# Tails of three weight units by token block ahead of two more layers, a scaled input in halves, norm weights moved into weights

## What is computed

```python
# first block, twice: x += 0.5*ffn(norm(x)); x += mixer(norm(x)); x += 0.5*ffn(norm(x))
#   first mixer: Mamba-2 ("mamba"), second: latent attention ("mla")
def _short_conv_mixer(h, w_in, w_conv, w_out):          # layer "conv"
    u = h @ w_in                                        # 1024 -> 4 x 1024
    b_gate, c_gate, xin, g = jnp.split(u, 4, axis=-1)
    y = b_gate * _causal_depthwise_conv(c_gate * xin, w_conv)   # 3 taps along tokens
    return (y * jax.nn.silu(g)) @ w_out
# layer "conv":  x = x + _short_conv_mixer(_rmsnorm(x, norm_a), w_in_a, conv_a, w_out_a)
# layer "stick": kv = _rmsnorm(x, norm_kv) @ w_kv       # k, v: 2 x 512
#                q, g = split(_rmsnorm(x, norm_b) @ w_in_b)
#                o = stick_breaking_attention(q, k, v)  # 8 heads of 64
#                x = x + (o * silu(g)) @ w_out_b
# end:           return _rmsnorm(x, norm_f)
def _rmsnorm(x, g):
    return x * rsqrt(mean(x * x) + eps) * g
```

## Time and profile before

| | |
|---|---|
| median of three runs | 1408.57 us (1407.95 to 1410.07) |
| profiled execution, its own time | 1409.99 us |
| its span in the trace | 1408.2 us |
| mean granted clock of PE | 0.968 of full |
| PE busy | 1327.6 us, 94% |
| DVE, ACT, POOL busy | 772.2, 673.6, 132.9 us |
| weights read | 216.82 MB, 155 GB/s over the span |

### The profile page before, as it was taken

How to read it: one execution, slowest core, us unless ns; L and a number is a source line. 1 busy time by engine, 2 the same in 40 slices (tenths; PEclk the granted TensorE clock), 3 DMA queues, 4 the chain that set the end, 5 groups by cost and what they waited for, 6 DMA issues and landing times.

```text
span 1408.2 us, 18444 instructions
## 1 busy us (share of the span) xinstructions
PE 1327.6 (94%) x7004; PEld 1130.8 (80%) x7004; DVE 772.2 (55%) x918; ACT 673.6 (48%) x878; POOL 132.9 (9%) x224
## 2 busy tenths in 40 slices
PE   6999999998889999999999998789999998997977
PEld 5888878997668888888888887678888878996965
DVE  4655545778656555545555445555555545664552
ACT  5544446664546544435444437545554334434441
POOL 3000001036540000000000004500000000000000
PEclk9999999999889999999999999989999999998989
DMA  8665534552125555563655634041755664653301
GB/s 277 196 192 190 202 120 152 179 179 87 63 90 187 172 179 179 179 231 116 221 179 181 232 121 150 30 121 60 239 179 179 209 179 120 180 180 120 120 1 45
DMA packets 179726, 218.78 MB, mean 155 GB/s; under 512 B 8553, under 2 KB 132782, under 8 KB 179662
## 3 DMA queue, kind: packets, MB, share of 16 engines
q1 hardware_dynamic: 179374, 217.75, 47.7%
q0 software_dynamic: 288, 0.15, 0.1%
HBM read 216.82 MB, written 1.05 MB: 155 GB/s over the span
## 4 chain that ended last, share of the span: by engine, by line
PE 85%; DVE 6%; ACT 4%; issue 2%; POOL 2%; DMA 0%; SPq 0%; POOLq 0%; ACTq 0%; DVEq 0%
PE acc L559 26%; PE acc L561 25%; PE acc L560 25%; PE tr L576 3%; DVE w_lo L1668 2%; ACT w_hi L1173 1%; ACT xT_hi L1181 1%; PE tr L807 1%; PE aux L949 1%; DVE conv L1864 1%; DVE xT_lo L1677 1%; DVE E L1822 0%; DMA raw<-in_ffn_w_up 0%; PE aux L1065 0%; PE aux L1066 0%
## 5 line engine op out<-in xcount | busy, mean ns | idle before, releaser
L1668 DVE TENSOR_TENSOR w_lo<-raw,w_hi 128x2048 fp32r<-128x2048 f32 (+1 forms) x207 | 465.8, 2278 | 212.7 <-ACT w_hi L1173 212.7
L1173 ACT ACTIVATE w_hi<-raw 128x2048 fp32r<-128x2048 f32 (+1 forms) x207 | 385.5, 1901 | 135.5 <-PE acc L561 126.9
L559 PE MATMUL acc<-w_hi,xT_hi 128*128 128x512 f32 (+1 forms) x898 | 361.8, 403 | 19.1 <-DVE hT_lo L1677 8.0
L561 PE MATMUL acc<-w_hi,xT_lo 128*128 128x512 f32 (+1 forms) x898 | 354.1, 394 | 0.0
L560 PE MATMUL acc<-w_lo,xT_hi 128*128 128x512 f32 (+1 forms) x898 | 353.8, 394 | 0.0
L559 PEld LDWEIGHTS acc<-w_hi,xT_hi 128*128 128x128 f32 x898 | 173.4, 193 | 55.3 <-DVE hT_lo L1677 8.5
L561 PEld LDWEIGHTS acc<-w_hi,xT_lo 128*128 128x128 f32 x898 | 172.5, 192 | 36.6
L560 PEld LDWEIGHTS acc<-w_lo,xT_hi 128*128 128x128 f32 x898 | 173.6, 193 | 33.6
L559 PE MATMUL acc<-w_hi,hT_hi 128*128 128x512 f32 x448 | 176.4, 394 | 3.4 <-DVE hT_lo L1677 2.6
L560 PE MATMUL acc<-w_lo,hT_hi 128*128 128x512 f32 x448 | 175.1, 391 | 0.0
L561 PE MATMUL acc<-w_hi,hT_lo 128*128 128x512 f32 x448 | 175.1, 391 | 0.0
(11 more groups left out here) (277 smaller groups left out, 1226.4 us busy)
## 6 DMA issues: line engine op xcount, KB each, us to landing
raw<-in_ffn_w_gate SPq DMA_DIRECT2D x88, 512.0 KB, 4.3
raw<-in_ffn_w_up SPq DMA_DIRECT2D x88, 512.0 KB, 5.5
raw<-in_ffn_w_down SPq DMA_DIRECT2D x88, 512.0 KB, 4.8
raw<-in_ssm_w_in SPq DMA_DIRECT2D x48, 512.0 KB, 4.7
raw<-in_w_in_a SPq DMA_DIRECT2D x64, 256.0 KB, 4.1
raw<-in_ssm_w_out SPq DMA_DIRECT2D x16, 512.0 KB, 4.3
raw<-in_mla_w_out SPq DMA_DIRECT2D x8, 512.0 KB, 4.6
raw<-in_w_out_a SPq DMA_DIRECT2D x8, 512.0 KB, 4.7
```

The source lines that it names most:

```text
L559: pe.matmul(o, lh, rh, start=start, stop=False, skip_group_check=skip)
L561: return pe.matmul(o, ll, rh, start=False, stop=stop, skip_group_check=skip)
L1173: act.activation(w_hi[:, u % RING, 0:n], raw[:, u % RING, 0:n], ACT.Copy).then_inc(hi_ready, 1)
L1668: dve.tensor_tensor(w_lo[:, u % RING, 0:n], raw[:, u % RING, 0:n], w_hi[:, u % RING, 0:n].bitcast(F32), ALU.subtract).then_inc(lo_ready, 1)
```

## The change

- `SCALED` = mamba, conv, stick. What held for mamba now holds for all three: `deep` is 3 ahead of them, the turn of block 0 stands before the last part of the tail, DVE takes the low parts of block 0 in its `sums`, one half behind each block's residual, and ACT splits the next layer's second unit between the squares and the scaling of block 0.
- `xn` is written in two instructions of 512 for each block, and PE's turn waits for each half by itself (mamba too).
- conv's first step is computed by token block, as tokens by features (`token_unit`, 48 matmuls of 512 columns, in `first_step`). ACT copies the results from the accumulators to `ct`, PE transposes `ct` back (eight transposes, between the two units of step f = 1), ACT copies one half and DVE the other to `ft`, and f = 1's convolution reads `ft`.
- stick's inputs are transposed without norm weights, one instruction of 512 for each half on ACT and on DVE. The norm weights go into the weights: of stick's first eight units (`w_kv`, `w_in_b`) ACT writes `w_hi` in four instructions of 512 with a column as scale, DVE `w_lo` in four.

```diff
+SCALED = ("mamba", "conv", "stick")
+def weight_norm(u):
+    n = u - sum(len(UNITS_OF[name.rstrip("0123")]) for name in PHASES[:-1])
+    return None if not 0 <= n < 8 else (NORM_KV, NORM_B)[n // 4] + 4 * (n % 2)
...
# PE, input_turns
-                        if half == 0:
-                            c.scaled += 1
-                            pe.wait_ge(xn_ready, c.scaled)
+                        c.scaled += 1
+                        pe.wait_ge(xn_ready, c.scaled)
# PE, first_step
+                k = c.turn - 2
                 early = unscaled(c.name)
-                k = c.turn - 2 if early else c.turn
-                if not early:
-                    input_turns(c.name, 0)
# PE, sum_units
-                deep = 3 if c.next == "mamba" else 2
+                deep = 3 if c.next in SCALED else 2
...
-                    if (n, tb) == (n_u - 1, 1) and (c.next == "mamba" or c.next != "end" and unscaled(c.next)):
+                    if (n, tb) == (n_u - 1, 1) and c.next != "end":
                         input_turns(c.next, 0)
# PE, short_conv
+                first_step(lambda half, tb: token_unit(c.unit + half, c.pair, 4 * half, 4, KD, 512, tbs=(tb,),
+                                                       done=tb == 1, mark=first_half if half else None))
...
+                        if f == 1 and half == 0:
+                            for tb in range(TB):
+                                acc_done(pe, p_first, tb)
+                                turn([(g * P, ct[:, tb, g * P:(g + 1) * P]) for g in range(4)], c.turn)
+                                c.turn += 1
# ACT, split
-                act.activation(w_hi[:, u % RING, 0:n], raw[:, u % RING, 0:n], ACT.Copy).then_inc(hi_ready, 1)
+                    for k in range(4):
+                        at = slice(512 * k, 512 * k + 512)
+                        inst = act.activation(w_hi[:, u % RING, at], raw[:, u % RING, at], ACT.Copy, scale=col(norm + k))
# ACT, layer_input
-                        if tb == 0 and c.name == "mamba":
+                        if tb == 0:
                             split_to(c.unit + 2)
                         act.wait_ge(rstd_ready, c.norm)
-                            act.activation(xn[:, tb, :], x[:, tb, :], ACT.Copy, scale=rstd[:, tb:tb + 1])\
+                        for half in range(2):
+                            at = slice(512 * half, 512 * half + 512)
+                            act.activation(xn[:, tb, at], x[:, tb, at], ACT.Copy, scale=rstd[:, tb:tb + 1])\
# ACT, short_conv
+                for tb in range(TB):
+                    if tb:
+                        act.wait_ge(unit_used, c.unit + 2)
+                    else:
+                        act.wait_ge(first_half, 1)
+                    acc_free(act.activation(ct[:, tb, :], bank(c.pair, tb), ACT.Copy), c.pair, tb)
+                    split_to(c.unit + 4)
...
+                    if f == 1:
+                        k = c.turn
+                        act.wait_ge(turned, k + 1)
+                        turn_free(act.activation(ft[:, :, 0:P], heads(tr[:, k % 2, :], 4), ACT.Copy), k)
+                        turn_done(act, k)
+                        turn_done(act, k + 1)
+                        c.turn += 2
+                        act.activation(g_sb[:], ft[:, 3, :], ACT.Silu).then_inc(gate_ready, 1)
# DVE, split
+                    for k in range(4):
+                        at = slice(512 * k, 512 * k + 512)
+                        inst = dve.scalar_tensor_tensor(w_lo[:, u % RING, at], raw[:, u % RING, at], col(norm + k),
+                                                        w_hi[:, u % RING, at].bitcast(F32), ALU.mult, ALU.subtract)
# DVE, sums
-                    elif c.next == "mamba":
+                    elif c.next in SCALED:
                         if tb == 0:
                             split_to(c.unit + 2)
                         input_low(c.next, 0, (tb,))
# DVE, short_conv
+                        if f == 1:
+                            k = c.turn
+                            dve.wait_ge(turned, k + 2)
+                            turn_free(dve.tensor_copy(ft[:, :, P:T], heads(tr[:, (k + 1) % 2, :], 4)), k + 1)
+                            c.turn += 2
+                            dve.wait_ge(gate_ready, f)
+                            turn_done(dve, k)
+                            turn_done(dve, k + 1)
+                            link(dve.tensor_tensor(v_sb[:], ft[:, 2, :], ft[:, 1, :], ALU.mult))
```

More of the change, by code:

```diff
@@ L86, in input_norms @@
         return (ffn_norm(int(name[3])),)
-    return {"mamba": (norm_col(0, 1),), "mla": (norm_col(1, 1),), "conv": (NORM_A,),
-            "stick": (NORM_KV, NORM_B)}[name]
+    return {"mamba": (norm_col(0, 1),), "mla": (norm_col(1, 1),), "conv": (NORM_A,)}[name]
+def weight_norm(u):
+    n = u - sum(len(UNITS_OF[name.rstrip("0123")]) for name in PHASES[:-1])
+    return None if not 0 <= n < 8 else (NORM_KV, NORM_B)[n // 4] + 4 * (n % 2)
 def unscaled(name):
@@ L637, in token_unit @@
                     last.then_inc(unit_used, 1)
+                elif mark:
+                    last.then_inc(mark, 1)
             def feature_unit(u, p, k0, source=(xT_hi, xT_lo), s0=0):
@@ L1094, in stick @@
                     for half in range(2):
-                        if n == 1:
+                        if n:
                             feature_unit(c.unit + half, c.pair, 4 * half)
-                        elif n > 1:
-                            feature_unit(c.unit + half, c.pair, 4 * half, (hT_hi, hT_lo), 8)
                         if n == 3:
@@ L1188, in input_high @@
                     act.wait_ge(turned, c.turn + 1)
-                    for norm, (dst, _, s0) in zip(input_norms(c.name), inputs_to):
+                    if c.name == "stick":
+                        act.activation(xT_hi[:, 4 * half:4 * half + 4, tb * P:(tb + 1) * P],
+                                       heads(tr[:, c.turn % 2, :], 4), ACT.Copy).then_inc(turn_hi, 1)
+                    else:
+                        (norm,) = input_norms(c.name)
                         for j in range(4):
-                            high(dst[:, s0 + 4 * half + j, tb * P:(tb + 1) * P], j * P, c.turn,
+                            high(xT_hi[:, 4 * half + j, tb * P:(tb + 1) * P], j * P, c.turn,
                                  col(norm + 4 * half + j), j == 3)
@@ L1218, in layer_input @@
                         split_to(2 * tb + 2)
-                    if tb and c.name == "mamba":
+                    if tb and c.name in SCALED:
                         split_to(c.unit + 3)
@@ L1228, in sums @@
                 c.pair += 2
-                split_to(c.unit + (1 if c.next == "mamba" else 2))
+                split_to(c.unit + (1 if c.next in SCALED else 2))
             def ffn(f):
@@ L1682, in input_low @@
             def input_low(name, tb, halves=(0, 1)):
-                norms = input_norms(name)
                 for half in halves:
-                    c.high += len(norms)
+                    c.high += 1
                     dve.wait_ge(turn_hi, c.high)
-                    for n, (norm, (hi, lo, s0)) in enumerate(zip(norms, inputs_to)):
+                    if name == "stick":
+                        at = (slice(None), slice(4 * half, 4 * half + 4), slice(tb * P, (tb + 1) * P))
+                        turn_free(dve.tensor_tensor(xT_lo[at], heads(tr[:, c.turn % 2, :], 4), xT_hi[at].bitcast(F32),
+                                                    ALU.subtract), c.turn)
+                    else:
+                        (norm,) = input_norms(name)
                         for j in range(4):
-                            at = (slice(None), s0 + 4 * half + j, slice(tb * P, (tb + 1) * P))
-                            low(lo[at], hi[at], j * P, c.turn, col(norm + 4 * half + j),
-                                j == 3 and n == len(norms) - 1)
+                            at = (slice(None), 4 * half + j, slice(tb * P, (tb + 1) * P))
+                            low(xT_lo[at], xT_hi[at], j * P, c.turn, col(norm + 4 * half + j), j == 3)
                     c.turn += 1
             def layer_input():
-                if not unscaled(c.name) and c.name != "mamba":
-                    input_low(c.name, 0)
                 if c.unit == 0:
```

66 lines of the change are left out of this document (36 added, 30 removed).

## The result

The changed kernel takes 1398.17 us (median of 20 executions, 1395.11 to 1415.04) beside 1409.58 us for the kernel before (20 executions, 1405.70 to 1411.62): a ratio of 0.9941 with an interval of 0.9923 to 0.9958. It is faster, as forecast, but by 11.4 us where 17.7 were forecast, and outside the stated range. Of the 20 executions 16 lie between 1395.1 and 1400.3, and four between 1411.1 and 1415.0; the kernel before had no such second group (of its 73 executions beside the later runs, one took 1428.4 us and the others at most 1413.0). The profiled execution took 1397.09 us with a span of 1395.4, 12.8 us less than before's 1408.2.

The account below looks back on a forecast made before the run. PE, busy for 94% of the span, bounds the kernel, so time is won only where it waits or runs at half clock. Gains 5.8 (conv) + 11.5 (stick) + 0.35 (mamba) = 17.7 us give 1390.9 us; range 1388.3 to 1394.6.

Parts of the forecast that it names:

- conv: pause ahead of block 1: At conv's entry, behind block 1's transposes, PE pauses about 1.9 us for the first low parts.
- conv: tail to second step: From the end of the tail's matmuls to conv's second step: 15.0 us against 22.44, a gain of 7.4.
- conv: transposes of `ct`: In conv's step f = 1, eight more transposes cost 1.04 us, all on PE's path.
- conv: wait for `w_lo`, once: Ahead of conv's f = 2, PE waits 0.6 us for unit 4's `w_lo`, without recurring.
- stick: wait for `xn`: At stick's early turn, `xn` is late by 0.5 us because of the scaled split on ACT.
- stick: pause ahead of block 1: At stick's entry, PE pauses 1.1 us and goes on 2.1 us after block 1's turn starts.
- stick: tail to second step: From the tail's end to stick's second step: 14.6 us against 26.16, a gain of 11.5.
- both entries together: At conv's and stick's entries, gains of 5.8 and 11.5 us, 17.3 in all.
- mamba's wait for `xn`: At mamba's entry, `xn` in halves removes the 0.39 us wait: gain 0.35, between 0.2 and 0.4.
- rival (a): Clock falls in the remaining entry pauses, 1.7 us lost each: 1392.6 for one, 1394.3 for both; chance 0.13.
- pieces of `w_hi`, `w_lo` with scale: In stick's scaled splits, pieces take about 0.6 us for `w_hi` and 0.68 us for `w_lo`.
- "unchanged" behind stick's second step: What follows stick's second step is unchanged, so nothing is gained or lost there.

Follow-up runs that it names:

- fill_tail2: fill_after with the tail ahead of conv and stick back at two units, early turn kept; 1405.60 us.
- fill_by_feature: fill_after with conv's first step by features for both blocks, without the turn of `ct`; 1414.97 us.
- fill_one_xn: fill_after with `xn` written in one instruction for each block again; 1393.03 us, one execution.
- fill_after: Changed kernel with 30 matmuls, results overwritten, in PE's pause ahead of the loop of heads; 1390.10 us, ratio 0.9864.
- fill_after2: fill_after run again without edit; 1388.45 us, ratio 0.9856.
- fill_before: Kernel before the change with 30 matmuls, results overwritten, in the pause ahead of the loop of heads; 1406.03 us, ratio 0.9979.
- keep_after: fill_after with two more matmuls of 512 columns in each of six heads of the loop; 1394.56 us, ratio 0.9894.
- before + 8: Kernel before the change with eight matmuls of 512 columns more ahead of stick's fourth step; 1407.99 us, ratio 0.9994.
- changed + 8: Changed kernel with eight matmuls of 512 columns more ahead of stick's fourth step; 1412.29 us, ratio 1.0019.

## Why the prediction was right and wrong

| step of the prediction | forecast | trace |
|---|---|---|
| conv: early turn beyond its matmuls | 1.1 | 1.14 |
| conv: pause ahead of block 1 | 1.9 | 1.95 |
| conv: tail to second step | 15.0 | 15.2 |
| conv: transposes of `ct` | 1.04 | 1.04 |
| conv: wait for `w_lo`, once | 0.6 | 0.65 |
| stick: wait for `xn` | 0.5 | 0.61 |
| stick: pause ahead of block 1 | 1.1 | 0.98 |
| stick: tail to second step | 14.6 | 14.8 |
| both entries together | 17.3 | 16.9 |
| mamba's wait for `xn` | 0.35 | 0.39, by putting it back |
| half clock at the entries, rival (a) | none | none |
| pieces of `w_hi`, `w_lo` with scale | 0.6, 0.68 | 0.71, 0.75 |
| four pieces of `w_hi` in a row | 2.4 | 2.56 |
| "unchanged" behind stick's second step | 0 | 6.0 us lost |

(16.9 is 22.44 - 15.2 for conv, less 1.04 and 0.65, and 26.16 - 14.8 for stick.) The entries hold. What the earlier trace rows gave for mamba could be carried to conv and stick, and the price of a piece with scale was 0.07 to 0.11 us short; of that at most the 0.11 us by which stick's wait for `xn` is longer than forecast reached the path. That 18.8 and not 17.7 us were won by stick's second step has its reason ahead of the change: the changed kernel's trace was 2.1 us ahead at the end of conv's tail (1159.20 against 1157.08), with only 0.39 of it from the change. The rest of the lead is scatter, and without it the sum closes: 16.9 + 0.4 - 6.0 = 11.3 us, beside 11.4 by the medians.

The Trainium skill, "TensorE: Matmul & The Clock Gate", section "Wait — 56ns, not 53.3ns?", would have made the two shapes of the product equal. The trace has 24 matmuls of 512 columns in 1163.68 - 1158.22 = 5.46 us, 0.2275 us each, and steps by features at 11.52 us as before, so it disagrees with the rule here and agrees with the rows that the sum went by.

**The step that failed** is the assumption in two sentences: "Neither work nor order changes outside these two stretches and mamba's entry" and "What follows stick's second step is unchanged". Of PE's work they are true (on ACT and DVE the scaled splits go on behind the second step, and the 45.6 us to the loop show that PE never waited for them); of its time they are false. Behind the pause for `zn` stands a stage that PE runs at half or at full clock, with a factor of 6.50 / 3.55 between them, and how many of its heads fall on which side depends on when it is entered. The kernel before stood at a favourable place with 9.9 us of half clock; the change put it at one with 22.9. 6.0 of 18.8 us went that way in the usual execution, and by the times more in four of 20. The warning stood in the trace of before: the granted clock of the loop was 0.81 over 26 us, and its heads had two durations. I read the clock only at the entries that the change touches. Rival (a) had the right mechanism at the wrong place and, with 1.7 to 3.4 us, at too small a price; no rival let it act behind the change. Its 3.4 us at half clock for each entry were worked out from no row; fill_tail2, where the clock did fall at both, has 3.4 us at each.

**What is not settled**: what fixes the instants at which the clock falls in or behind a pause, and rises again inside a stage in which PE is always busy. The runs show a relation of the fall in the pause to the entry, for seven traces, and that with the pause filled the clock fell in the loop in three traces (fill_tail2, fill_by_feature, fill_one_xn) and not in four (fill_after, fill_after2, fill_before, keep_after). All seven have the wait of 1.5 us for `wt`, which ends 7.1 us behind the entry, and the three falls came 0.5 to 1.7 us behind it; why there and not in the other four is open. No trace shows a fall in the loop without it, and no run took that wait away. Whether another order of the heads' matmuls would make the stage robust was not tried.

## What to carry to other kernels

Before pricing a change at "nothing downstream", list the granted clock of every stage behind it; where a stage runs partly at half clock, or follows a long pause, the gain is uncertain by the stage's difference between the two levels (here up to 8 x 2.95 us), in both directions. To measure a change apart from that, compare both kernels with the pause ahead of the stage filled, and read times from a common point in the traces instead of from the start. Filling such a pause with matmuls whose result nobody reads cost nothing that these runs show and won 8 to 10 us in the changed kernel, so it belongs to the change, but it has to be looked at again after every edit that shifts the stage.

## What the runs showed of the hardware

- PE at 26.00 of 26.00 us busy stayed at half clock, and in one kernel for about 49 of the 50.4 us of its eight heads. The heads' matmuls use 64 or 128 rows and 128 or 256 columns with no row of waiting between them; being busy by the profile was not enough to bring the clock back. The Trainium skill, "TensorE: Matmul & The Clock Gate", section "HAM oscillation — how this bites in real kernels", puts falls of the clock down to idle gaps of PE and advises to keep it at work. The filled pause agrees (0.56 became 1.00 over the loop's first 26 us); the fall at 1354 us in fill_by_feature, in a stretch with 29.96 of 30 us busy and with its last gap of 1.5 us just before, shows that the gap need not be a long one here.
- A shift of 0.4 us between the fall and the entry separated 4.7 us of half clock (before + 8) from a loop of 50.4 us, nearly all at half clock (changed + 8), one trace each. More work could make the kernel faster: 1.4 us added, 4.9 us less time.
- The same pause length does not give the same clock: 1.95 us at conv's entry kept 1.00 in the changed kernel, while in fill_tail2 the same pause (1.96 us), with one of 2.32 us twelve us ahead of it, had the fall behind it (0.79 over the 8 us from 1168).
- Stages untouched by the change move an execution as well: from 200 to 430 us the mean clock was between 0.93 and 0.96 in the traces of kernels whose code is the same up to conv's entry, and that entry came within 7.1 us. A difference of 0.03 over these 230 us is by itself worth 6.9 us, as an estimate from these figures.
